# Moving the shared region of stage buffers in SBUF from 32 bytes past a multiple of 64 to a multiple of 128

## The chip, the cores and the metric

The kernel runs on one core of a Trainium2 chip. Its time is the device time of one execution in microseconds (us); lower is better. The engines are named as in the profile: PE is TensorE's matmul, PEld its loading of the stationary operand, DVE is VectorE, ACT is ScalarE, POOL is GpSimd and SP issues the weight transfers. SBUF is the on-chip memory from which all of them read, PSUM the one into which PE writes.

## What is computed

A network of three layers on one sequence of 512 tokens of width 1024, all in float32. A hybrid layer (a chunkwise mLSTM with 4 heads beside three-branch sparse attention with 8 heads, merged through gates) is followed by a feed-forward block. The second part has two layers, each with a feed-forward block before and after its mixer: the even one mixes with a gated MLP over token chunks and with differential attention, the odd one with latent attention and grouped-query attention. In outline:

```
x = x + merge(mlstm(rms(x) @ w_in), nsa(rms(x) @ w_in)) @ w_out
a, v = split(rms(x) @ ffn_w_up)
x = x + (gelu(conv(a)) * v) @ ffn_w_down
for l in range(2):
    x = x + 0.5 * swiglu(rms(x), ffn1_w_gu[l], ffn1_w_down[l])
    x = x + mixer[l](rms(x)) @ w_out[l]
    x = x + 0.5 * swiglu(rms(x), ffn2_w_gu[l], ffn2_w_down[l])
```

The five feed-forward blocks go from 1024 to 2 x 2816 columns and from 2816 back to 1024.

## The kernel before, in words

Activations lie transposed, with features on the 128 partitions and the 512 tokens along the row, so that a tile of 128 features is [128, 512] float32, or 2048 bytes in a row. Every large product is made from float32 numbers split into a high and a low part of type fp32r: `three(l, r)` pairs the high weights with the high and then the low part of the moving side, and the low weights with its high part, so one tile of 128 input features costs three matmuls of 512 columns, all added in one PSUM bank.

The weights come from memory in the order of `weight_plan`, one piece at a time, mostly 8 tiles of 128 x 128 (512 KB). SP fetches a piece into one of four slots of `WF`, ACT writes its high part into `WH` (L292) and DVE the low part into `WL` (L295). `project` then runs over the tiles `k` of the input: a tile of `WH` or `WL` is the stationary operand, and the moving operand is

- `HH` and `HL`, the two parts of the normed activations, where the input is the residual stream: all input projections and all up-projections of the feed-forward blocks;
- `AH` and `AL` (ten seats each) in the down-projections of the feed-forward blocks, in chunks of 8, 8 and 6 tiles;
- `YH`/`YL`, `MXH`/`MXL`, `O2H`/`O2L` with `O3H`/`O3L`, and `HMH`/`HML`, `ONH`/`ONL` in the output projections of the mixers.

In the profile a matmul is named ps<-A,B with its two operands in the order of the alphabet, not of their roles. With ps<-AH,WH the moving operand is AH. Where a product is made by tokens, `WH` moves and `HH` is stationary (ps<-WH,HH). Each matmul has a load of its own stationary operand (LDWEIGHTS), which runs beside the matmul ahead of it. Line 284 is the helper that records nearly all matmuls.

Storage is laid out by hand. `put` gives each tensor the next free place, at a multiple of 32 bytes. X, HH, HL, WF, WH, WL, C (the constants), PR, SC (ten scratch rows of 516 numbers), SM, LM, R and RT come first and live through the whole program. What is left is the region in question: `base` is its start, and `arena(name, kb, ...)` puts a tensor at `base + kb * 1024`. The stages use it in turn, so that tensors of different stages overlap. The addresses that follow from the code are these (offset in each partition, in bytes):

```
                    address    mod 64   mod 128
X                     16512         0         0
HH, HL         32896, 49280         0         0
WH, WL         82048, 94336         0         0
C                    106624         0         0
RT (16 bytes)        138752         0         0
base, AH             138784        32        32
```

After RT the next free place is 138784. All tensors of the region lie at a multiple of 64 bytes past `base`, the large ones at whole KB, so each of them begins 32 bytes past a multiple of 64, and so does every 2048-byte tile in them.

```
        def put(name, shape, at=None, dt=F32):
            n = 4 * int(np.prod(shape[1:]))
            if at is None:
                at = place["at"]
                place["at"] += (n + 31) // 32 * 32
...
        AH = arena("AH", 0, [128, NA, S], F32R)
        AL = arena("AL", 2 * NA, [128, NA, S], F32R)
```

Order of work: each engine has its program written out, in the same order of stages; semaphores tell the others what is ready. Nothing in the order depends on an address.

Of the kernel before, what the change touches and what calls it, by code (L numbers as in the profile page):

```python
# [617 lines left out]
def build(nc, xT, wall, par, cst, late, latep, out):  # L618
# [9 lines left out]
    with ExitStack() as ctx:  # L628
# [3 lines left out]
        place = {"at": (nc.sbuf_base + 63) // 64 * 64}  # L632
# [6 lines that stand above are left out]
            assert at + n <= nc.sbuf_usable_end, (name, at + n, nc.sbuf_usable_end)  # L639
            return nc.alloc_sbuf_tensor_at(name, shape, dt, offset=at)  # L640
# [12 lines left out]
        LM = put("LM", [128, 12])  # L653
        R = put("R", [128, S])
        RT = put("RT", [128, 4])
        base = place["at"]
        KB = 1024

        def arena(name, kb, shape, dt=F32):
# [1970 lines left out]
```

How the kernel before makes its waits and increments, by code:

```python
    def then_inc(self, *_):  # L266
        return self
# [8 lines left out]
    def wait_ge(self, sem, n):  # L276
        if self.real is not None and self.met.get(id(sem), 0) < n:
            self.met[id(sem)] = n
            self.real.wait_ge(sem, n)
# [778 lines left out]
        def sync_program(e):  # L1058
            at = 0
            for n, (_, _, _, r, c) in enumerate(plan):
                if n >= NWF:
                    e.wait_ge(*w_low[n - NWF])
                    if plan[n - NWF][0] in ("c2k", "c2v"):
                        e.wait_ge(*projected[n - NWF])
                w = len(r) // 128 * len(c)
                e.dma_start(WF[:, n % NWF, 0:w], wall[at:at + 128 * w].rearrange("(p n) -> p n", p=128))\
                 .then_inc(s_slot[n % NWF], 16)
                at += 128 * w
# [2 lines left out]
            def project(n, o, moving, made, M=128):  # L1071
                wh, wl = wview(WH, n, NWS), wview(WL, n, NWS)
                e.wait_ge(*w_low[n])
                for k in range(len(moving)):
                    for w in made(k):
                        e.wait_ge(*w)
                    for i, (l, r) in enumerate(three((wh[:, k, 0:M], wl[:, k, 0:M]), moving[k])):
                        done = e.matmul(o, l, r, k == 0 and i == 0, k == len(moving) - 1 and i == 2)
                done.then_inc(*projected(n))
# [1 line left out]
            def from_h(s, n, ph, kind, key, M=128):  # L1082
                for w in bank_left(ph, kind, key):
                    e.wait_ge(*w)
                project(n, bank(ph, kind, key)[0:M, :], hs, lambda k: [h_low[s, k]], M)
```

## Time and profile before

| | before |
|---|---|
| median of 3 runs | 3077.14 us (3077.13 to 3078.55) |
| the profiled execution, its own time | 3077.35 us |
| its span, first to last instruction | 3075.6 us |
| PE busy | 2897.7 us, 94% of the span |
| DVE busy | 1665.1 us, 54% |
| ACT busy | 1142.9 us, 37% |
| POOL busy | 184.8 us, 6% |
| mean granted clock of TensorE | 0.969 of full |

A matmul's duration in the profile runs from its start to the modelled end, and consecutive matmuls overlap in it: what one costs on a busy PE is the distance between two starts, which the durations follow but do not equal. The granted clock has two levels, full (2.4 GHz) and half (1.2 GHz).

### The profile page before, as it was taken

The page shows a single profiled execution, that of the slowest core. Times are in us where ns is not written, and L with a number is a line of the kernel's source. Part 1 is how long each engine was busy: PE and PEld are TensorE (multiplying, and loading weights), DVE is VectorE, ACT ScalarE, POOL GpSimd, SP SyncE. Part 2 cuts the span into 40 slices and gives each one's busy share as a digit, 9 for nine tenths or more (in the row PEclk, how much of TensorE's full clock was granted, in tenths as well). Part 3 has the DMA queues.
Part 4 walks back from the last instruction along what each step waited for, and adds up shares of the span by engine and source line. Part 5 has one row for each costly group of instructions (what it writes and reads, how often), then busy time and mean ns, then how long its engine had stood idle before and what let it go on. Part 6 is the DMA issues. An engine that isn't in the chain of part 4 may idle for free.

```text
span 3075.6 us, 33674 instructions
## 1 busy us (share of the span) xinstructions
PE 2897.7 (94%) x13182; PEld 2360.8 (77%) x13182; DVE 1665.1 (54%) x2508; ACT 1142.9 (37%) x1766; POOL 184.8 (6%) x178
## 2 busy tenths in 40 slices
PE   6987899999999999999789999999999887799999
PEld 5776678888887888887678888888887665688887
DVE  6586644564555444446954343543444987643433
ACT  4455533322223222343633222322223776432322
POOL 1012310000000000001200000000000321000000
PEclk9988899999999999999899999999999999999999
DMA  3111013332322323232012332232221010123232
GB/s 125 62 43 43 10 59 99 105 102 92 97 86 99 97 96 93 86 96 69 14 62 89 96 96 92 93 97 96 96 88 62 29 42 21 35 90 101 91 95 83
DMA packets 70542, 240.50 MB, mean 78 GB/s; under 512 B 7888, under 2 KB 9808, under 8 KB 70128
## 3 DMA queue, kind: packets, MB, share of 16 engines
q1 hardware_dynamic: 68112, 230.85, 23.5%
q0 software_dynamic: 1120, 5.39, 0.5%
q8 instruction: 106, 1.74, 0.2%
q10 hardware_dynamic: 1152, 2.10, 0.2%
q14 instruction: 52, 0.43, 0.0%
HBM read 236.21 MB, written 2.10 MB: 77 GB/s over the span
## 4 chain that ended last, share of the span: by engine, by line
PE 85%; DVE 10%; issue 3%; ACT 2%; POOL 0%; DMA 0%; DVEq 0%; ACTq 0%; POOLq 0%
PE ps L284 83%; DVE SC L307 2%; DVE SM L313 2%; PE ps L287 1%; DVE SC L295 1%; DVE PTL L295 1%; ACT SC L292 1%; DVE SC L301 1%; DVE WL L295 0%; DVE SC L310 0%; DVE SM L321 0%; DMA PR<-par 0%; POOL SC L302 0%; DVE EQ L295 0%; DVE SC L302 0%
## 5 line engine op out<-in xcount | busy, mean ns | idle before, releaser
L284 PE MATMUL ps<-HH,WH 128*128 128x512 f32 (+1 forms) x2192 | 862.3, 393 | 14.2 <-DVE HL L307 13.7
L284 PE MATMUL ps<-HL,WH 128*128 128x512 f32 (+1 forms) x2192 | 858.2, 392 | 0.0
L284 PE MATMUL ps<-HH,WL 128*128 128x512 f32 (+1 forms) x2192 | 857.7, 391 | 0.0
L295 DVE TENSOR_TENSOR WL<-WF,WH 128x1024 fp32r<-128x1024 f32 (+2 forms) x473 | 545.6, 1158 | 423.5 <-ACT WH L292 422.7
L292 ACT ACTIVATE WH<-WF 128x1024 fp32r<-128x1024 f32 (+2 forms) x473 | 467.5, 994 | 723.7 <-PE ps L284 723.6
L284 PEld LDWEIGHTS ps<-HH,WH 128*128 128x128 f32 (+1 forms) x2192 | 414.8, 189 | 102.8 <-issue 14.7
L284 PEld LDWEIGHTS ps<-HH,WL 128*128 128x128 f32 (+1 forms) x2192 | 413.9, 189 | 88.1
L284 PEld LDWEIGHTS ps<-HL,WH 128*128 128x128 f32 (+1 forms) x2192 | 414.7, 189 | 86.6
L284 PE MATMUL ps<-AH,WH 128*128 128x512 f32 x880 | 349.8, 397 | 3.5 <-DVE AL L295 3.5
L284 PE MATMUL ps<-AH,WL 128*128 128x512 f32 x880 | 349.5, 397 | 0.0
L284 PE MATMUL ps<-AL,WH 128*128 128x512 f32 x880 | 349.3, 397 | 0.0
L295 DVE TENSOR_TENSOR X<-X,ps 128x512 f32<-128x512 f32 x144 | 99.1, 688 | 292.5 <-PE ps L284 292.5
L292 ACT ACTIVATE SC<-SC 128x512 f32<-128x512 f32 (+2 forms) x157 | 98.0, 624 | 334.7 <-DVE SC L295 176.0
L284 PEld LDWEIGHTS ps<-AH,WH 128*128 128x128 f32 x880 | 166.1, 189 | 45.0 <-DVE AL L295 4.8
L284 PEld LDWEIGHTS ps<-AL,WH 128*128 128x128 f32 x880 | 166.2, 189 | 40.4
L284 PEld LDWEIGHTS ps<-AH,WL 128*128 128x128 f32 x880 | 166.0, 189 | 40.5
L292 ACT ACTIVATE AH<-SC 128x512 fp32r<-128x512 f32 x110 | 69.5, 632 | 300.0 <-DVE SC L295 300.0
L307 DVE SCALAR_TENSOR_TENSOR SC<-ps,R 128x512 f32<-128x512 f32 x88 | 60.8, 691 | 208.4 <-PE ps L284 208.4
L287 PE MATMUL ps<-C,SC 128*128 128x128 f32 (+1 forms) x560 | 100.0, 301 | 73.9 <-POOL SC L302 27.2
L295 DVE TENSOR_TENSOR SC<-ps,R 128x512 f32<-128x512 f32 x176 | 119.8, 686 | 84.9 <-PE ps L284 71.3
L284 PEld LDWEIGHTS ps<-C,SC 128*128 128x128 f32 (+2 forms) x872 | 119.8, 207 | 45.1 <-issue 17.9
L287 PEld LDWEIGHTS ps<-C,SC 128*128 128x128 f32 (+1 forms) x560 | 69.6, 150 | 105.0 <-DVE SC L301 35.6
(282 smaller groups left out, 3163.6 us busy)
## 6 DMA issues: line engine op xcount, KB each, us to landing
WF<-wall SPq DMA_DIRECT2D x397, 512.0 KB, 3.5
WF<-wall SPq DMA_DIRECT2D x40, 384.0 KB, 3.0
WF<-wall SPq DMA_DIRECT2D x17, 256.0 KB, 2.7
X<-xT ACTq DMA_DIRECT2D x8, 256.0 KB, 12.4
outT<-X POOLq DMA_DIRECT2D x8, 256.0 KB, 2.3
WF<-wall SPq DMA_DIRECT2D x4, 288.0 KB, 3.0
LT<-late POOLq DMA_DIRECT2D x1, 1152.0 KB, 5.5
LP<-latep POOLq DMA_DIRECT2D x1, 1024.0 KB, 7.2
```

The costliest lines, as they stand in the source:

```text
L284: return self.real.matmul(o, l, r, start=start, stop=stop, skip_group_check=True)
L287: return self.real.transpose(o, i, ident) if self.real is not None else Uncounted()
L292: return self.real.activation(o, i, func, bias=bias, scale=scale, accum_out=accum_out)
L295: return self.real.tensor_tensor(o, a, b, op) if self.real is not None else Uncounted()
L301: return self.real.tensor_scalar(o, a, s1, None, op0)
L307: return self.real.scalar_tensor_tensor(out=o, in0=a, scalar=s, in1=b, op0=op0, op1=op1)
L313: return self.real.tensor_reduce(o, i, AX.X, op, negate=negate) if self.real is not None else Uncounted()
```

## The change

`base` is rounded up to the next multiple of 128. It moves from 138784 to 138880, 96 bytes on, and every tensor of the region moves with it. The last one (EK11) ends at 228992 instead of 228896, and the end of usable SBUF is 229368. The tensors put ahead of the region keep their places. Each engine has the same instructions in the same order as before, with the same waits; only addresses of operands differ.

```diff
--- before.py
+++ after.py
@@ -653,7 +653,7 @@
         LM = put("LM", [128, 12])
         R = put("R", [128, S])
         RT = put("RT", [128, 4])
-        base = place["at"]
+        base = (place["at"] + 127) // 128 * 128
         KB = 1024
 
         def arena(name, kb, shape, dt=F32):
```

## Rows read from the trace of the kernel before

**Rows 1.** The page: span, busy time by engine, chain that ended last

```profile
span 3075.6 us, 33674 instructions
...
PE 2897.7 (94%) x13182; PEld 2360.8 (77%) x13182; DVE 1665.1 (54%) x2508; ACT 1142.9 (37%) x1766; POOL 184.8 (6%) x178
...
PE 85%; DVE 10%; issue 3%; ACT 2%; POOL 0%; DMA 0%; DVEq 0%; ACTq 0%; POOLq 0%
PE ps L284 83%; DVE SC L307 2%; DVE SM L313 2%; PE ps L287 1%; DVE SC L295 1%; DVE PTL L295 1%; ACT SC L292 1%; DVE SC L301 1%; DVE WL L295 0%; DVE SC L310 0%; DVE SM L321 0%; DMA PR<-par 0%; POOL SC L302 0%; DVE EQ L295 0%; DVE SC L302 0%
```

**Rows 2.** Matmul groups by shape: busy us, mean ns | idle before, releaser

```profile
L284 PE MATMUL ps<-HH,WH 128*128 128x512 f32 x2184 | 859.1, 393 | 14.2 <-DVE HL L307 13.7 <-DVE WL L295 0.5
L284 PE MATMUL ps<-HL,WH 128*128 128x512 f32 x2184 | 855.0, 391 | 0.0
...
L284 PE MATMUL ps<-AH,WH 128*128 128x512 f32 x880 | 349.8, 397 | 3.5 <-DVE AL L295 3.5
L284 PE MATMUL ps<-AH,WL 128*128 128x512 f32 x880 | 349.5, 397 | 0.0
L284 PE MATMUL ps<-AL,WH 128*128 128x512 f32 x880 | 349.3, 397 | 0.0
...
L284 PE MATMUL ps<-WH,HH 128*128 128x512 f32 x96 | 37.4, 389 | 0.0
...
L284 PE MATMUL ps<-MXL,WH 128*128 128x512 f32 x64 | 25.6, 400 | 0.0
...
L284 PE MATMUL ps<-YH,WH 128*128 128x512 f32 x64 | 25.4, 396 | 0.0
...
L284 PE MATMUL ps<-O3L,WH 128*128 128x512 f32 x32 | 12.7, 397 | 0.0
...
L284 PE MATMUL ps<-HML,WH 128*128 128x512 f32 x32 | 12.7, 396 | 0.0
```

**Rows 3.** Line 284, 1186 to 1231 us: duration min/median/max, first and last start

```profile
L284 PEld LDWEIGHTS ps<-AH,WH x64: 187/188/192, 1186.0 to 1230.3; 128*128 128x128 f32 x64
L284 PE MATMUL ps<-AH,WH x64: 392/397/400, 1186.3 to 1230.5; 128*128 128x512 f32 x64
...
L284 PE MATMUL ps<-AL,WH x64: 392/397/400, 1186.5 to 1230.8; 128*128 128x512 f32 x64
```

**Rows 4.** The same view, PE alone, 1099.6 to 1185.9 us

```profile
L284 PE MATMUL ps<-HL,WH x128: 389/389/393, 1099.4 to 1185.8; 128*128 128x512 f32 x128
...
L284 PE MATMUL ps<-HH,WH x127: 389/389/389, 1099.9 to 1185.6; 128*128 128x512 f32 x127
```

**Rows 5.** Timeline of PE: start us, us, instruction, at three borders

```profile
1099.20 0.40 PE L284 MATMUL ps<-HH,WH 128*128 128x512 f32 x1
...
1186.25 0.40 PE L284 MATMUL ps<-AH,WH 128*128 128x512 f32 x1
...
1231.23 0.40 PE L284 MATMUL ps<-HH,WH 128*128 128x512 f32 x1
```

**Rows 6.** Windows: us, busy (instructions) by engine, granted clock, DMA share, GB/s

```profile
1099.00:1186.00 87.00, 87.00 (x385) 72.05 (x384) 39.65 (x46) 25.68 (x31) 0.00 (x0) 1.00 0.30 97
1186.00:1231.00 45.00, 45.00 (x194) 36.16 (x193) 16.70 (x18) 9.01 (x9) 0.00 (x0) 1.00 0.31 95
```

**Rows 7.** Timeline of PE: differential attention, probabilities times values

```profile
1494.40 0.39 PE L284 MATMUL ps<-PTH,BVH 128*128 128x512 f32 x1
...
1496.21 0.40 PE L284 MATMUL ps<-PTH,BVL 128*128 128x512 f32 x1
```

**Rows 8.** Groups of DVE and ACT by shape, columns as in group 2

```profile
L295 DVE TENSOR_TENSOR X<-X,ps 128x512 f32<-128x512 f32 x144 | 99.1, 688 | 292.5 <-PE ps L284 292.5
...
L295 DVE TENSOR_TENSOR AL<-SC,AH 128x512 fp32r<-128x512 f32 x110 | 76.2, 693 | 76.7 <-ACT AH L292 76.7
...
L292 ACT ACTIVATE AH<-SC 128x512 fp32r<-128x512 f32 x110 | 69.5, 632 | 300.0 <-DVE SC L295 300.0
...
L292 ACT ACTIVATE SC<-X 128x512 f32<-128x512 f32 x64 | 40.3, 630 | 153.6 <-DVE X L295 153.6
```

**Rows 9.** Waits, 1030 to 1300 us: us in total, times, longest

```profile
ACT WH L292 <- PE ps L284: 111.5, 32, 4.6
...
DVE X L295 <- PE ps L284: 47.9, 16, 3.3
```

## The prediction

> **What bounds the kernel now.** I read the page first. PE is busy for 94% of the span, and the chain of work that ended last runs through it for 85%, for 83% through the matmuls of line 284 alone [rows 1]. So what a matmul costs in a dense run decides the time, and an engine that is idle half of the time does not. The windows say the same of two stretches in the middle of a feed-forward block: PE is busy in every microsecond of both, at full clock, while DVE has work for 39.65 of 87 us in the one and for 16.70 of 45 us in the other [rows 6]. Among the longest waits of that part of the program are those of ACT and DVE for PE, 111.5 and 47.9 us [rows 9].
>
> Then I looked for a place in which the trace already shows operands on either side of this change. There is one, because the program mixes both kinds of address all the time. HH and HL lie at a multiple of 128 bytes. AH and AL lie in the region, 32 bytes past a multiple of 64. Both are moved against the same stationary slots WH and WL, through the same code, with the same shape and three matmuls to a tile. The groups by shape give 397 ns for each of the three kinds with AH or AL, and 393 and 391 ns for those with HH and HL, whose means also hold the stretches at half clock [rows 2]. In clean stretches it is sharper: a median of 397 ns and never under 392 for AH and AL [rows 3], 389 ns in nearly every one of 128 for HL and 389 in all of 127 for HH [rows 4].
>
> Durations overlap, so the cost is read from starts. From the first matmul of an up-projection stretch at 1099.20 us to the first one of the down-projection at 1186.25 us there are 384 matmuls (8 tiles of inputs, 3 matmuls each, 16 pieces): 87.05 / 384 = 226.7 ns each. From there to 1231.23 us there are 192 (8 x 3 x 8 pieces): 44.98 / 192 = 234.3 ns each [rows 5]. The difference is 7.6 ns for a matmul, or 3.3%. At the granted clock of 1.00 in both windows [rows 6] that is some 18 cycles of 2.4 GHz.
>
> Two things say that it follows the address and not the role. First, it is there for every other moving tensor of the region, in other stages, beside other work: means of 400 ns for MXL, 396 for YH, 397 for O3L and 396 for HML, each against WH [rows 2]. Second, the pair HH and WH, both outside the region, doesn't have it with the roles exchanged either, where WH moves and HH is stationary (389 ns) [rows 2].
>
> A third group tells something of how it comes about. In differential attention the moving operand PTH and the stationary BVH and BVL are both in the region. From 1494.40 to 1496.21 us there are 8 steps: 1.81 / 8 = 226 ns [rows 7]. So a moving operand at 32 past 64 is not slow in itself. Slow is a moving operand at 32 past 64 with a stationary one at 0, or the reverse: a matmul streams 512 columns while the load of the next tile reads its own 128. I take this as the working theory: the pair costs 7.6 ns when the two lie differently within 64 (or 128) bytes, and nothing when they lie alike.
>
> **The change part by part.** It adds and removes no instruction, no wait and no transfer, and moves no instruction on any engine, PE's, SP's and POOL's queues included. What it does is give all tensors of the region the place within 128 bytes that HH, WH and C have.
>
> Matmuls with a moving operand in the region and a stationary one in WH or WL. The down-projections have 880 x 3 = 2640 [rows 2]; that is 22 tiles x 8 outputs x 3 in each of five blocks. The output projections of the two later layers and of the merge have 8 x 8 x 3 = 192 each, so 576, and the two up-projections of the merge (HM and ON, 4 tiles each) 96 each, so 192. Sum: 3408. If each falls from 234.3 to 226.7 ns, that is 3408 x 7.58 = 25.8 us. The bounds of this price: nothing if the difference is not of the address, and 7.58 ns at most, since the aligned pairs never go below 226.7 in a dense stretch. I take the upper end, since the changed operands will lie exactly as HH does (their addresses agree even in their remainder by 256, which is 128 for both).
>
> Does all of it reach the end of the kernel? In the down-projection stretch PE has no idle time, and DVE and ACT have 28 and 36 us of the 45 free [rows 6]. The most that they could be asked for is known too: after the change a down-projection piece takes as long as an up-projection piece takes now, 24 x 226.7 = 5.44 us, and up-projections run at that pace with more DVE work in a microsecond (39.65 / 87 = 0.46 against 16.70 / 45 = 0.37) and the same transfer rate of 95 to 97 GB/s [rows 6]. So nothing that fed PE comes late. Only at the 3.5 us in which PE waits for AL [rows 2] is another engine the one that ends last, and those stay. I count nothing as given back.
>
> Loads of stationary operands: 188 ns with AH's matmuls [rows 3], and 72.05 / 384 = 188 ns in the other window [rows 6]. They lie beside the matmuls and I count zero. If they were uncovered they would not differ.
>
> Matmuls with both operands in the region (scores, probabilities times values): alike before and alike after, zero by the theory. There are about 400 wide ones, so if they gained too, it would be 400 x 7.6 = 3.0 us. That is the one bound on the gain's side.
>
> DVE, ACT and POOL: writes into the region or reads from it. DVE takes 693 ns with AL and AH and 688 ns with X, ACT 632 ns into AH and 630 ns from X [rows 8]. These are within 1% across the two kinds of address, and the engines have slack: zero. What covers it is the idle time in group 6; without it, 110 x 5 ns = 0.6 us.
>
> The sum: against the profiled execution 3077.35 - 25.8 = 3051.5 us (its span 3075.6 - 25.8 = 3049.8, and 1.75 us lie around it). Its own time is 0.2 us above the median of the three runs, so for the median 3077.14 - 25.8 = 3051.3 us.
>
> **The rivals.**
>
> *The moving operand's own place counts* (were the operand read 64 bytes at a time, a 2048-byte row that begins 32 past would take 33 reads instead of 32: 226.7 x 33 / 32 = 233.8 ns, which is close to the 234.3). Then the roughly 400 wide matmuls inside the region gain as well: 25.8 + 3.0, so 3048.3 us. Against it stand the 226 ns of group 7, with PTH at 32 past 64. Chance 0.07.
>
> *A part of it.* The relation is by something finer than I think, or half of the matmuls keep a step of 230 ns: 12.9 us, so 3064 us. Nothing in the trace asks for it. Chance 0.08.
>
> *No difference*, 3077 us: the 7.6 ns belong to the tensors' roles. For it speaks that no row shows AH at an aligned place. Against it speaks that five kinds of tensor (A, MX, Y, O and HM), written and used in different stages, all have it. Chance 0.08.
> The Trainium skill speaks for this rival in two places. SBUF — State Buffer, in Door 1: The DMA port swizzle, gives SBUF lines of 16 bytes to read from; 32 past 64 is the start of such a line as much as 0 is, so by that rule alone the sum would be 0 and the time 3077 us. TensorE: Matmul & The Clock Gate, also of the Trainium skill, says under Step-by-step: what each phase is for that PE has "two independent SBUF read ports", so that a load takes nothing from the matmul beside it, which would again give 0. This trace does not agree with either as a full account: 234.3 against 226.7 ns with nothing else different but the tensor.
>
> *Slower.* What collides may be any two accesses that lie alike, and not only PE's own. ACT and DVE write AH and AL while PE streams HH and HL in the up-projections; today these lie at different places within 64 bytes, after the change at the same. If that costs PE the same 7.6 ns in all 6840 matmuls with HH or HL, it is 51.8 us, less the 25.8: 3103 us. It decides from 25.8 us / 6840 = 3.8 ns a matmul on. Against it: in the windows of group 6 DVE and ACT already write WH, WL and X, all at multiples of 128, while PE reads HH and WH at multiples of 128 for 226.7 ns. Chance 0.03.
>
> **How the numbers follow.** The forecast as summed has 0.74. Its own range is 3048 to 3055 us: the three runs of before differ by 1.4 us, and some matmuls around borders between stages or at half clock gain a little more or less than 7.6 ns. The range to 3046 below takes in the rival with 3 us more, to 3060 above the better part of a partial gain; beyond it are no difference, the worse partial cases and slower, together under 0.2. Faster by over 0.2% (6 us, about what a measurement of this kernel tells from no change) holds the forecast, the first rival and the partial gain: 0.89. Same 0.08, slower 0.03.
>
> **What the profile of the changed kernel would show.** Right: the median of AH's and AL's matmuls in a down-projection stretch is 389 ns instead of 397, a stretch of 192 starts takes 43.5 us instead of 45.0, HH's stay at 389, PTH against BVH stays at 226 ns from start to start, DVE's and ACT's means stay, and each feed-forward block is shorter by 4 us (528 matmuls x 7.6 ns). Wrong: AH still at 397 (the role, not the place); AH at 389 but PE idle ahead of it, with a releaser in WL (the weights come late); HH's median above 389 (the slower rival). A change of the granted clock's share could also move the time by a few us either way, since the mean is 0.969.

## The result and the profile after

| | before | after |
|---|---|---|
| median on the same chip | 3077.14 us (3076.49 to 3078.55, 4 runs) | 3043.76 us (3042.94 to 3048.91, 4 runs) |
| ratio | | 0.9894, 95% interval 0.9877 to 0.9912 |
| the profiled execution | 3077.35 us | 3042.94 us |
| its span | 3075.6 us | 3041.1 us |
| mean granted clock | 0.969 | 0.972 |

The change makes the kernel 1.1% faster, 33.4 us. The prediction was wrong: it forecast a gain of 25.8 us, to 3051.3 us, with 3046 us as its lower end, and the measured time lies below that.

The page after shows who gave the time. These lines answer to [rows 1]:

```profile
span 3041.1 us, 33674 instructions
PE 2862.1 (94%) x13182; PEld 2348.3 (77%) x13182; DVE 1663.6 (55%) x2508; ACT 1142.6 (38%) x1766; POOL 184.9 (6%) x178
PE 84%; DVE 10%; ACT 3%; issue 3%; POOL 0%; DMA 0%; DVEq 0%; ACTq 0%; POOLq 0%
```

PE's busy time fell by 35.6 us, the span by 34.5; DVE, ACT and POOL have the same work and the chain has the same shape. The groups by shape of the changed kernel, for [rows 2]:

```profile
L284 PE MATMUL ps<-HH,WH 128*128 128x512 f32 x2184 | 856.8, 392 | 14.6 <-DVE HL L307 14.2 <-DVE WL L295 0.5
...
L284 PE MATMUL ps<-AH,WH 128*128 128x512 f32 x880 | 342.7, 389 | 3.9 <-DVE AL L295 3.9
L284 PE MATMUL ps<-AL,WH 128*128 128x512 f32 x880 | 342.4, 389 | 0.0
L284 PE MATMUL ps<-AH,WL 128*128 128x512 f32 x880 | 342.3, 389 | 0.0
...
L284 PE MATMUL ps<-YH,WH 128*128 128x512 f32 x64 | 25.0, 391 | 0.0
L284 PE MATMUL ps<-MXL,WH 128*128 128x512 f32 x64 | 25.1, 393 | 0.0
```

All kinds with a moving operand in the region have come down to what HH has, and PE's wait for AL is still there (3.9 us). The first two groups of [rows 8] show DVE and ACT unmoved in the changed kernel:

```profile
L295 DVE TENSOR_TENSOR X<-X,ps 128x512 f32<-128x512 f32 x144 | 98.9, 687 | 270.3 <-PE ps L284 270.2
L295 DVE TENSOR_TENSOR AL<-SC,AH 128x512 fp32r<-128x512 f32 x110 | 76.2, 693 | 76.8 <-ACT AH L292 76.8
```

The same stretch as in [rows 5 and 6], on the changed kernel's timeline of PE and then in its windows (columns as there):

```profile
1090.04 0.39 PE L284 MATMUL ps<-HH,WH 128*128 128x512 f32 x1
...
1177.08 0.39 PE L284 MATMUL ps<-AH,WH 128*128 128x512 f32 x1
...
1220.60 0.39 PE L284 MATMUL ps<-HH,WH 128*128 128x512 f32 x1
```

```profile
1090.00:1177.00 87.00, 87.00 (x385) 72.03 (x385) 39.65 (x46) 25.68 (x31) 0.00 (x0) 1.00 0.31 97
1177.00:1220.50 43.50, 43.50 (x194) 36.02 (x193) 16.70 (x18) 9.01 (x9) 0.00 (x0) 1.00 0.31 97
```

The down-projection stretch takes 43.52 / 192 = 226.7 ns a matmul instead of 234.3, the up-projection one 87.04 / 384 = 226.7 as before. From one down-projection stretch to the start of the second layer (1054.23 to 1330.25 us before, 1046.52 to 1318.52 after), with 528 affected matmuls in it, the time falls from 276.02 to 272.00 us: 4.02 us, and 528 x 7.6 ns = 4.01. Products inside the region stay as they were, here from start to start in 1.13 / 5 = 226 ns:

```profile
1481.46 0.39 PE L284 MATMUL ps<-PTH,BVL 128*128 128x512 f32 x1
...
1482.59 0.39 PE L284 MATMUL ps<-PTL,BVH 128*128 128x512 f32 x1
```

So the term of 25.8 us came very nearly as summed; only in the first feed-forward block did the step of the two full down-projection stretches fall by less, from 239.2 to 232.5 ns. What came beside it is seen when the start of the same instruction is compared in both traces, piece by piece. Five pieces gained clearly more than their matmuls explain. Four hold a pause of PE between two stages, in which DVE works out the norm (the releaser is DVE SC L310), and the first one a pause of 2.08 us in which PE waits for AL:

| piece, starts before | before | after | fell by | matmuls in it x 7.58 ns | rest |
|---|---|---|---|---|---|
| 924.85 to 1054.23 | 129.38 | 126.87 | 2.51 | 144: 1.09 | 1.42 |
| 1330.25 to 1378.47 | 48.22 | 46.59 | 1.63 | 0 | 1.63 |
| 1607.05 to 1698.81 | 91.76 | 90.11 | 1.65 | 0 | 1.65 |
| 1974.83 to 2066.61 | 91.78 | 90.11 | 1.67 | 0 | 1.67 |
| 2702.82 to 2794.60 | 91.78 | 90.11 | 1.67 | 0 | 1.67 |

The rests add up to 8.04 us. The span fell by 34.5 us, so 8.7 us stand beside the 25.8: these 8.04, 1.3 us from the start of the second layer's mixer to that of its output projection (2342.63 to 2657.46 us before, 2316.46 to 2629.96 after), and -0.7 for all the rest. (1.5 us gained before 92 us, where the inputs arrive, are lost again by 126 us.) What happens in such a piece is on the timeline of PE (start us, us, instruction, and in brackets idle time and releaser). First the kernel before, at the pause that is the second row of the table:

```profile
1354.08 1.83 PE L284 MATMUL ps<-C,SC 128*128 128x128 f32 x8 [1.10 <-DVE SC L310]
1355.56 0.77 PE L284 MATMUL ps<-HH,WH 128*128 128x512 f32 x1
1356.14 0.63 PE L284 MATMUL ps<-HL,WH 128*128 128x512 f32 x1
...
1358.07 0.39 PE L284 MATMUL ps<-HH,WH 128*128 128x512 f32 x1
```

and the same instructions in the changed kernel:

```profile
1340.29 0.95 PE L284 MATMUL ps<-C,SC 128*128 128x1 f32 x8
1342.33 1.16 PE L284 MATMUL ps<-C,SC 128*128 128x128 f32 x8 [1.10 <-DVE SC L310]
1343.24 0.47 PE L284 MATMUL ps<-HH,WH 128*128 128x512 f32 x1
1343.56 0.39 PE L284 MATMUL ps<-HL,WH 128*128 128x512 f32 x1
...
1344.71 0.39 PE L284 MATMUL ps<-HH,WH 128*128 128x512 f32 x1
```

The idle time is 1.10 us in both, with the same releaser. Before, a stretch of 3.4 us at half clock (1.2 GHz) follows, in which matmuls take 0.63 to 0.77 us; after, none does. From the 8 small matmuls ahead of the pause (1352.04 before) to the seventh matmul behind it are 6.03 us against 4.42. In the feed-forward blocks from 900 us on, the kernel before has six such stretches (931, 976, 1354, 1621, 1989 and 2716 us) and the changed one two (969 and 2331, the second at a pause that is clean before). The one at 931 us is not at a norm but behind the wait for AL, where the changed kernel has a pause of 2.19 us and no stretch. In the kernel before:

```profile
930.60 0.50 PE L284 MATMUL ps<-AH,WH 128*128 128x512 f32 x1 [2.08 <-DVE AL L295]
...
931.18 0.63 PE L284 MATMUL ps<-AH,WL 128*128 128x512 f32 x1
```

### The profile page after: what moved, and what is told of

It reads as the page before. It is cut to its first block, busy times and chain, and to the rows that moved or that the text cites. A ratio compares the mean times of both kernels' runs of the same rounds, so it can differ in the third digit from the quotient of the medians.

```text
span 3041.1 us, 33674 instructions
## 1 busy us (share of the span) xinstructions
PE 2862.1 (94%) x13182; PEld 2348.3 (77%) x13182; DVE 1663.6 (55%) x2508; ACT 1142.6 (38%) x1766; POOL 184.9 (6%) x178
## 4 chain that ended last, share of the span: by engine, by line
PE 84%; DVE 10%; ACT 3%; issue 3%; POOL 0%; DMA 0%; DVEq 0%; ACTq 0%; POOLq 0%
PE ps L284 83%; DVE SC L307 2%; DVE SM L313 2%; PE ps L287 1%; DVE PTL L295 1%; DVE SC L295 1%; ACT SC L292 1%; DVE SC L301 1%; DVE WL L295 1%; DVE SC L310 0%; DVE SM L321 0%; DMA PR<-par 0%; POOL SC L302 0%; DVE EQ L295 0%; DVE SC L302 0%
## 5 line engine op out<-in xcount | busy, mean ns | idle before, releaser
L284 PE MATMUL ps<-AH,WH 128*128 128x512 f32 x880 | 342.7, 389 | 3.9 <-DVE AL L295 3.9
L284 PE MATMUL ps<-AL,WH 128*128 128x512 f32 x880 | 342.4, 389 | 0.0
L284 PE MATMUL ps<-AH,WL 128*128 128x512 f32 x880 | 342.3, 389 | 0.0
L284 PEld LDWEIGHTS ps<-C,SC 128*128 128x128 f32 (+2 forms) x872 | 115.6, 201 | 45.1 <-issue 18.7
```

The source lines that it names most:

```text
L284: return self.real.matmul(o, l, r, start=start, stop=stop, skip_group_check=True)
```

## The experiments

Two questions are open: what exactly must agree for the 226.7 ns, and where the 7.6 us beyond the sum (33.4 - 25.8) are from. The stretch borders named below are read as in [rows 5], as the start of the first matmul with HH, of the first with AH and of the next with HH; the stretches have 384 and 192 matmuls. The remainders are those of the tensors' addresses, which all their tiles, 2048 or 512 bytes apart, share modulo 512. Diffs are against the changed kernel.

**The changed kernel again**, on another chip.

> The changed kernel once more, to see how its time scatters. It was 33.4 us faster than before where 25.8 us were forecast from the distance between starts. Theory A (the rest is the clock): the matmul intervals alone give 25.8 us, and what is above that is the number of stretches at half clock, which differs from one execution to the next; then the executions spread over 3043 to 3051 us and the time falls as the mean granted clock rises, by about 1.6 us for each isolated half-clock stretch of 3.4 us. Theory B (the placement also speeds up something else, such as the attention stages): all executions lie within 2 us of 3043.5 us, at whatever mean clock.

Measured: 3048.18 us (3042.33 to 3051.99, 4 runs) against 3077.57 (16 runs); ratio 0.9902, interval 0.9889 to 0.9916. The gain of about 1% stands. The executions spread over 9.7 us, the fastest with a mean granted clock of 0.971 and the slowest with 0.968, as theory A has it and not B. The profiled execution is the one of 3048.18. In its trace the last down-projection stretch starts 28.07 us earlier than in the kernel before, where in the first trace it was 33.33. Of these 5.3 us, 2.0 arise before 542 us, and most of the others in the second layer's attention, where a stretch of 10 us at half clock stands at 2445 us that the first trace doesn't have.

**Stationary slots 32 bytes on, with the region alike to them.** WH, WL and AH at 160 modulo 256, HH and HL at 128.

```diff
+        place["at"] += 32
         WH = put("WH", ...)
         WL = put("WL", ...)
+        place["at"] += 96
...
-        base = (place["at"] + 127) // 128 * 128
+        base = place["at"]
```

> From the kernel before, the region stays 32 bytes past a multiple of 64, HH and HL stay at a multiple of 128, and only WH and WL are moved to 32 past. Theory of the pair (slow if moving and stationary operand lie differently within 64 bytes): AH against WH now lie alike and cost 226.7 ns from start to start, HH against WH lie differently and cost 234.3 ns; 6840 x 7.6 - 3408 x 7.6 = +26 us, so 3103 us. Rival, the moving operand's own place: HH moves at 226.7 ns and AH at 234.3 ns as before, 3077 us, with the stationary operand's place without effect.

Measured: 3088.13 us (3086.63 to 3091.48, 5 runs), ratio 1.0033, interval 1.0021 to 1.0045. Line 284 in the two stretches (minimum, median, maximum in ns, first and last start):

```profile
L284 PE MATMUL ps<-HH,WH x128: 394/396/397, 1102.1 to 1191.0; 128*128 128x512 f32 x128
...
L284 PE MATMUL ps<-AH,WH x64: 388/389/396, 1191.7 to 1234.5; 128*128 128x512 f32 x64
```

The roles have changed sides. HH, which has not moved, is now slow (89.60 / 384 = 233.3 ns), and AH, at 32 past 64 as in the kernel before, is fast (43.54 / 192 = 226.8). It is the pair that counts and not the moving operand's own place; that rival falls, and so does the one that gave the 7.6 ns to the tensors' roles. The price is 6.6 ns here instead of 7.6: 6840 x 6.6 = 45.1 us, less 25.8, is +19 us against before; measured are 11 us. The trace has only two stretches at half clock in the feed-forward blocks from 900 us on (978 and 1361), where the kernel before has six.

**Everything 32 bytes on.** All of X, HH, HL, WH, WL and the region at 160 modulo 256.

```diff
+        place["at"] += 32
         X = put("X", ...)
...
-        base = (place["at"] + 127) // 128 * 128
+        base = place["at"] + 96
```

> From the kernel before, everything is moved by 32 bytes and the region starts 32 past a multiple of 128, so that X, HH, HL, WF, WH, WL, C and the whole region all lie 32 past a multiple of 64. Theory of the pair: all pairs lie alike, all wide matmuls cost 226.7 ns, 3044 to 3051 us, as fast as the changed kernel although nothing large is at a multiple of 64. Rival, the moving operand's own place: all 10,248 wide matmuls at 234.3 ns, 3077 + 6840 x 7.6 = 3129 us.

Measured: 3043.07 us (3042.45 to 3045.6, 4 runs), ratio 0.989, interval 0.9874 to 0.9905, the same as the change.

```profile
L284 PE MATMUL ps<-AH,WH x64: 389/389/389, 1177.5 to 1220.3; 128*128 128x512 f32 x64
```

226.7 ns in both stretches (87.04 / 384 and 43.52 / 192). No operand lies at a multiple of 128 or of 64 in this kernel, and it loses nothing. "A multiple of 128" is not the property that pays.

**The region at a multiple of 64 only.** AH at 64 modulo 256, WH at 128.

```diff
-        base = (place["at"] + 127) // 128 * 128
+        base = (place["at"] + 63) // 64 * 64
```

> The region starts 64 past a multiple of 128 instead of at a multiple of 128; the rest is as in the changed kernel. If the pair must lie alike within 64 bytes: AH against WH at 226.7 ns from start to start, 3044 to 3051 us as the changed kernel. If it must lie alike within 128 bytes: AH against WH at 234 ns or more, 3070 us or more.

Measured: 3072.64 us (3071.01 to 3079.4, 11 runs), ratio 0.9985, interval 0.9977 to 0.9994.

```profile
L284 PE MATMUL ps<-AH,WH x64: 394/394/394, 1185.0 to 1229.1; 128*128 128x512 f32 x64
```

44.80 / 192 = 233.3 ns. Agreement within 64 bytes doesn't do: 6.6 of the 7.6 ns are left.

**The region at the next multiple of 128.** AH at 0 modulo 256, WH at 128.

```diff
-        base = (place["at"] + 127) // 128 * 128
+        base = (place["at"] + 127) // 128 * 128 + 128
```

> The changed kernel with the region 128 bytes further on: still a multiple of 128, but now at 0 within 256 bytes where HH, HL, WH and WL are at 128. If lying alike within 128 bytes is enough, AH against WH costs 226.7 ns from start to start, 3043 to 3052 us. If it takes 256 bytes, 233 ns or more and 3070 us or more.

Measured: 3070.34 us (3067.82 to 3071.97, 10 runs), ratio 0.9977, interval 0.9968 to 0.9986.

```profile
L284 PE MATMUL ps<-AH,WH x64: 392/394/398, 1183.2 to 1227.3; 128*128 128x512 f32 x64
```

44.80 / 192 = 233.3 ns again. This kernel does what the change says in words, a region at a multiple of 128, and gains 7 us instead of 33; of the 7, 3408 x 1.0 ns = 3.4 us are the step, and it has three of the half-clock stretches of 930 to 2708 us where the kernel before has six (and one at 602 us that the kernel before doesn't have). Agreement within 128 bytes isn't enough either.

**256 bytes further than the change.** AH at 128 modulo 256 like WH, but at 384 modulo 512, where WH has 128.

```diff
-        base = (place["at"] + 127) // 128 * 128
+        base = (place["at"] + 127) // 128 * 128 + 256
```

> The changed kernel with the region 256 bytes further on. In all placements so far AH against WH cost 226.7 ns from start to start where their addresses agree modulo 512 (the changed kernel, everything at 32, WH and WL at 32 beside the region at 32), and 233 to 234 ns where they differ by 32, 64, 96 or 128 modulo 256; the three fast ones agree modulo 256 as well. Theory: they have to agree modulo 512, which is the length of a row of the stationary tile (128 numbers of 4 bytes); then AH against WH costs 230 ns or more here, 3056 to 3072 us. Rival: modulo 256 is enough; then 226.7 ns and 3043 to 3052 us.

Measured: 3043.96 us (3041.79 to 3046.58, 4 runs) against 3075.04; ratio 0.99, interval 0.9884 to 0.9917.

```profile
L284 PE MATMUL ps<-AH,WH x64: 389/389/389, 1177.4 to 1220.3; 128*128 128x512 f32 x64
```

43.52 / 192 = 226.7 ns. Agreement modulo 256 is enough, and agreement modulo 512 isn't asked for.

**HL alone 32 bytes on.** The edit was to put HL at another place than HH.

```diff
+        place["at"] += 32
         HL = put("HL", ...)
+        place["at"] += 96
         WF = put("WF", ...)
```

> The changed kernel with only HL moved to 32 bytes past a multiple of 128; HH, WH, WL, C and the region stay at a multiple of 128. In each tile of an up-projection the three matmuls are HH against WH, HL against WH, HH against WL. If only the matmul whose own moving operand lies differently pays, one in three costs 233 to 234 ns: 2280 x 7 = +16 us over the changed kernel, 3060 to 3066 us. If a change of place from one moving operand to the next costs as well, two or three in three pay and it is 3075 us or more. Rival, the pair is not what counts: no change.

Measured: 3058.96 us (3058.42 to 3063.44, 4 runs), ratio 0.9946, interval 0.993 to 0.9961. The run doesn't isolate what it was meant to: the two shifts move WH, WL and AH on by 128 bytes to 0 modulo 256, so HH (128) is unlike them too. The down-projections, all at 0, have 226.8 ns (43.54 / 192). The up-projections have 87.92 / 384 = 229.0 ns, 2.3 more than alike, although none of their three pairs agrees modulo 256:

```profile
L284 PE MATMUL ps<-HH,WH x128: 387/392/395, 1094.7 to 1182.0; 128*128 128x512 f32 x128
L284 PE MATMUL ps<-HL,WH x128: 391/391/398, 1095.0 to 1182.2; 128*128 128x512 f32 x128
L284 PE MATMUL ps<-HH,WL x127: 388/388/400, 1095.2 to 1181.8; 128*128 128x512 f32 x127
```

HH is 128 bytes from W here, as AH is with the region at the next multiple of 128, where the step was 233.3 ns. So the price is not always 6.6 ns and does not follow from one pair's difference alone; what sets it is open.

**WL alone 32 bytes on.** WH, HH and AH at 128 modulo 256, WL at 160: two of three matmuls have alike operands.

```diff
+        place["at"] += 32
         WL = put("WL", ...)
```

> The changed kernel with only WL moved by 32 bytes; WH, HH, HL and the region stay. (C, SC and the small tensors behind WL move by 32 too.) In each tile the order is HH against WH, HL against WH, HH against WL, and the load of WL runs while HL's matmul streams. If the load that runs beside a matmul decides, the step from HL's matmul to the next one grows to 233 ns and the two others stay near 227. If a matmul's own stationary operand decides, it is the step from the matmul with WL to the next. Either way one in three of 10,248 pays 7 ns: +24 us over the changed kernel, 3070 us. If the two moving streams in a row had to lie alike and the stationary one did not count, nothing changes, 3046 us.

Measured: 3111.27 us (3105.82 to 3114.7, 4 runs), ratio 1.0118, interval 1.0095 to 1.0142. It was to cost a third of a full disagreement, some 24 us, and costs 67 us over the changed kernel. Both stretches have 233.3 ns (89.60 / 384 and 44.80 / 192), and 6840 matmuls with H and 3408 with operands of the region make 10,248 x 6.6 ns = 68 us. Line 284, and the timeline inside a down-projection:

```profile
L284 PE MATMUL ps<-AH,WH x64: 395/395/395, 1199.4 to 1243.5; 128*128 128x512 f32 x64
L284 PE MATMUL ps<-AL,WH x64: 400/400/400, 1199.6 to 1243.7; 128*128 128x512 f32 x64
L284 PE MATMUL ps<-AH,WL x64: 389/389/389, 1199.8 to 1243.9; 128*128 128x512 f32 x64
```

```profile
1209.87 0.40 PE L284 MATMUL ps<-AH,WH 128*128 128x512 f32 x1
1210.10 0.40 PE L284 MATMUL ps<-AL,WH 128*128 128x512 f32 x1
1210.34 0.39 PE L284 MATMUL ps<-AH,WL 128*128 128x512 f32 x1
1210.57 0.40 PE L284 MATMUL ps<-AH,WH 128*128 128x512 f32 x1
```

Three matmuls take 0.70 us instead of 0.68. The unrounded starts in this stretch give 239 ns from AL's matmul to the next, 233 ns from AH with WH and 228 ns from AH with WL: two of the three are slower, and the one whose own stationary operand is out of line is hardly slower than with everything alike (226 to 227 ns). The longest is the one with AL, during which the load of WL runs. That fits a cost that arises between a matmul and the load beside it, of the next stationary operand, at 12 ns and not the 7 that was expected. It does not explain why the one with AH and WH, both alike to what is loaded beside it, has 395 and 233.

**A few matmuls more, in both kernels.** To shift the pauses without touching an address, the first matmul of the first output projection (at about 545 us) is issued 8 times more in the changed kernel and 9 times more in the kernel before (whose `base` it keeps). Each is overwritten by the next, so nothing of the computation changes; by themselves they put all that follows some 2 us later. The question is whether the half-clock stretches hang on when a pause comes, or on how fast the matmuls ahead of it are.

```diff
+                        if n == piece["wo"][0] and k == 0 and i == 0:
+                            for _ in range(8):
+                                e.matmul(o, l, r, True, False)
```

> The changed kernel with eight matmuls more: the first one of the first output projection (at about 544 us) is issued nine times instead of once, each time starting its PSUM bank anew, so that the result is the same. All that follows comes 8 x 227 = 1.8 us later. Theory A (the part of the gain above 25.8 us is where the pauses of PE ahead of each norm fall in time, which decides whether the clock is halved for 3.4 us after them): the pauses of the later feed-forward blocks, after which the clock stayed up in three profiles of the changed placement (at 1341, 1604, 1966 and 2686 us), now draw half-clock stretches; time up by 1.8 us and 1.6 us for each of 2 to 4, so 5 to 8 us over the changed kernel, 3050 to 3053 us. Theory B (dense matmuls at 226.7 ns in the down-projection keep the clock up after the pause): the pauses stay clean, 1.8 us over the changed kernel.

> The kernel before with nine matmuls more in the same place (2.1 us of work, result unchanged), addresses as before. Theory A: the pauses at 976, 1354, 1621, 1989 and 2716 us, which were all followed by a half-clock stretch in the profile of before, are moved to where they draw none; the kernel gets faster by up to 5 x 1.6 - 2.1 = 6 us although it does more work, 3070 to 3073 us, while AH against WH stays at 234.3 ns. Theory B: the pauses behind slow matmuls keep their half-clock stretches, 3079.5 us.

Measured for the changed kernel: 3046.26 us (3044.24 to 3049.53, 4 runs), ratio 0.9901, interval 0.9887 to 0.9914; 2.5 us over the changed kernel's first median, which is near B's 1.8 and not the 5 to 8 that theory A had put. A half-clock stretch came at 604 us, and behind it the same two pauses as in the changed kernel are hit (972, 2334). For the kernel before: 3077.15 us (3073.19 to 3083.36, 11 runs), ratio 1.0006, interval 0.9997 to 1.0016. Its AH matmuls still have 234.3 ns (44.98 / 192), but the pauses at 973 and 1619 us are now clean, against theory B, and there are stretches at 602 and 1401 us that the kernel before didn't have. The one of 1619 us, which had 1.54 and 0.77 us for the two rows after the pause in the kernel before, on the timeline of the shifted one:

```profile
1618.07 0.95 PE L284 MATMUL ps<-C,SC 128*128 128x1 f32 x8
1620.12 1.16 PE L284 MATMUL ps<-C,SC 128*128 128x128 f32 x8 [1.10 <-DVE SC L310]
1621.04 0.47 PE L284 MATMUL ps<-HH,WH 128*128 128x512 f32 x1
```

So slow matmuls ahead of a pause aren't enough to bring the half clock, and a few matmuls more, with no change of address, move it from some pauses to others. How many are hit in the end was not forecast rightly by either theory. Nor was the shift the one that was meant: in the profiled execution the pauses of the kernel before with nine matmuls more come from 2.6 us earlier to 0.1 us later than in the first trace of the kernel before, and those of the changed kernel with eight more come 3.2 us later and further on 6.6, because half-clock stretches elsewhere came or went as well.

**Both kernels once more**, on one chip, to see whether the pattern belongs to the program.

> The kernel before, unchanged, for a second profile of it and more of its times. In the first profile six pauses of PE in the feed-forward blocks (at 931, 976, 1354, 1621, 1989 and 2716 us) were followed by 3.4 us at half clock; in three profiles of the changed placement only one or two were. If the placement of the pauses in time is a stable property of each kernel, the second profile shows four or more of them again and the time is 3075 to 3079 us. If it is chance in each execution, it shows another number, and the times of before spread as those of the changed kernel do, 3069 to 3084 us.

> The changed kernel, unchanged, for a third profile of it beside the one of before on the same chip. Stable property: one or two pauses of the feed-forward blocks at half clock again, 3042 to 3049 us, and 30 us or more under before. Chance: the difference to before goes towards the 25.8 us that the steps between matmuls alone give.

Measured: the kernel before 3076.85 us (3072.09 to 3079.7, 11 runs; ratio to its own runs 0.9999, interval 0.999 to 1.0007), the changed one 3044.11 us (3042.12 to 3045.91, 4 runs; ratio 0.9895, interval 0.988 to 0.991). The stretches of the first are at 933, 978, 1357, 1623, 1991 and 2718 us, the same six pauses; those of the second at 969 and 2330, the same two. The second row of the table above, in the kernel before:

```profile
1356.17 1.77 PE L284 MATMUL ps<-C,SC 128*128 128x128 f32 x8 [1.09 <-DVE SC L310]
1357.59 0.77 PE L284 MATMUL ps<-HH,WH 128*128 128x512 f32 x1
```

and in the changed one:

```profile
1341.88 1.16 PE L284 MATMUL ps<-C,SC 128*128 128x128 f32 x8 [1.10 <-DVE SC L310]
1342.80 0.47 PE L284 MATMUL ps<-HH,WH 128*128 128x512 f32 x1
```

**What all the traces say together.** Timing against pace can be settled from the clock records of the 14 traces. Each has seven pauses of 1.09 to 1.10 us after 500 us whose releaser is DVE SC L310 and after which the eight small matmuls of the norm start. A half-clock stretch follows 41 of these 98 pauses. In every trace the half-clock stretches of the whole program begin on one even raster, each within 0.002 us. Now take the time from the end of a pause (the start of its first small matmul) to the next point of that raster. For the 41 pauses that are hit it is 0.10 to 1.49 us; for the 57 that are spared it is 1.54 us or more, and 0.01 us once. There is no exception, with fast and with slow matmuls alike. At the pauses of the table (1354, 1620, 1988 and 2716 us) the kernel before has 0.30, 0.62, 1.48 and 0.51 us, and the changed kernel 2.06, 2.04, 1.76 and 2.22. The wait for AL of the table's first row, one in each trace, sorts in the same way: in six traces its end lies within 0.6 us of a point and a stretch begins there, in eight it lies 2.5 us or more ahead of one and none does. Of the seven pauses at norms the kernel before has five hit and the changed one two.

This also explains the last two pairs of runs. Two traces of the kernel before agree in this distance to 0.1 us at all seven pauses, although the second comes 2.1 us later by the program's own time; so do the three of the changed kernel up to 2400 us. With eight matmuls more the changed kernel's distances after 900 us differ from those of its first trace by at most 0.2 us, so that run was no test of another timing. With nine more, the pauses of the kernel before up to 1620 us moved (0.10 to 2.97, 0.30 to 1.39 and 0.62 to 2.43 us: two of these three spared; the one at 601 us to 1.01, now hit) and the later ones did not.

## Why the prediction was wrong, point by point

**What bounds the kernel**: right. PE still works in every microsecond of both windows, and what its matmuls lost the span lost.

**The price, 7.58 ns, and the count, 3408**: right in the main. The count leaves out 72 matmuls of CQ and CK against WH and WL (0.5 us at that price), and in the first block the price was 6.7 ns. Elsewhere the step fell from 234.3 to 226.7 ns, the medians from 397 to 389, and one clean block by 4.02 us against 4.01.

**"I count nothing as given back"**: right, as were the zeros for DVE, ACT and POOL and for the products inside the region (226 ns before and after).

**The term that was missing: the clock.** The step that failed is the sum's last one, from the 25.8 us of the steps straight to the time: it held the half-clock stretches equal, a term put at nothing without a reason. They stood only in the last paragraph as "a few us either way", and the forecast's own range had no more than 3.3 us below for them. In place of nothing they gave 8.04 us: five pieces without the stretch that they had before, each shorter by 1.42 to 1.67 us. The rows for it were in the trace of before: six pauses each followed by 3.4 us at half clock, at 1.6 us each, so up to 9.6 us that could be won by a shift, and two pauses of the norm without a stretch (603 and 2356 us) that could be hit. A lower end of 3051.3 - 9.6 = 3042 us would have held the result. Shown is that this part repeats: all kernels with 226.7 ns everywhere lie between 3043.07 and 3048.18 us (medians), under the 3051.3 of the sum. Shown too, by the kernel before with nine matmuls more, is that it can change without any address, and by the 98 pauses that the place of a pause in the raster of its trace decides it without exception. So this part is no gain of the placement as such: shorter matmuls moved the pauses, and five of them, hit before, ended up where none is hit, while one that was spared ended up where it is (2331 us). As far as the change goes, that was luck. What holds one program at the same places of the raster in each execution was not settled.

**The working theory**: right in kind, wrong in grain. The prediction said that the pair costs "when the two lie differently within 64 (or 128) bytes, and nothing when they lie alike". The pair it is: moving the stationary slots made HH slow and AH fast. But pairs that agree within 64 (multiple of 64) or within 128 (next multiple of 128) still take 233.3 ns, and only stretches in which all operands agree modulo 256 take 226.7 to 226.8 a matmul, wherever they lie. Nor is it the pair alone: with WL out of line a matmul whose own two operands agree still takes 233 ns to the next start. For this change nothing hung on it, because the address that it gives happens to agree with WH modulo 256, as the prediction noted. The differences tried in the down-projections, all operands of a kind together, are 96, 64 and 128 (slow: 234.3, 233.3, 233.3 ns) and 0 and 256 (fast); the up-projections add 32 (233.3).

**The rivals.** The moving operand's own place: refuted by AH's 226.8 ns at 32 past 64. No difference: refuted by the result. The SBUF lines of 16 bytes of the Trainium skill (SBUF — State Buffer, Door 1: The DMA port swizzle) do not show in these steps: two offsets that are both multiples of 16 differ by 7.6 ns. The sentence on two independent read ports (the Trainium skill, TensorE: Matmul & The Clock Gate, Step-by-step: what each phase is for) doesn't hold as a full account either: where only WL's address differs, the matmul beside its load is the one that goes from 389 to 400 ns. Partial: the price was full, but as the price of a badly chosen multiple of 128 it is real (7 us gained instead of 33). Slower: HH stays at 389 ns while ACT and DVE write at the same place modulo 256, so writes of others don't collide with PE's reads in this way.

## What to carry to other kernels

Place what a matmul moves and what it holds stationary alike modulo 256 bytes, all parts of one product together (one slot out of line slowed two of three matmuls, and cost as much as all out of line); "aligned to 128" is neither needed nor enough. Look for such a price by comparing starts of equal matmuls on tensors with different address remainders. And where a profile has stretches at half clock behind short pauses, count them and put their full worth into the range, since any change of the timing can deal them anew.

## What the runs showed of the hardware that was not expected

- The step of a 512-column fp32r matmul with a 128x128 load is 226.7 ns when all operands of the stretch agree modulo 256 and 233.3 to 234.3 in most placements where they don't, 16 to 18 cycles of 2.4 GHz. Why the kernel before, with a difference of 96, has 234.3 and those with 32, 64 and 128 have 233.3 is open.
- With WL alone out of line, the three kinds of matmul take 233, 239 and 228 ns to the next start, 233.3 on average; with H and W apart by 128 and 160 the average is 229.0. The relation of the price to the difference, and between successive matmuls, is open.
- The same pause of 1.10 us is followed by 3.4 us at half clock or not, 6.03 against 4.42 us. In 98 such pauses of 14 traces it was followed by it exactly when the pause ended 0.10 to 1.49 us ahead of a point of the raster on which that trace's half-clock stretches begin. Profiled again, the same program had it at the same pauses; with nine matmuls more it had it at others.
